# A norm whose second tile's products go ahead of the first tile's turning, and a mixer whose heads come out earlier and whose first result is turned by its roots

## The chip, the core and the metric

The kernel runs on one core of a Trainium2 chip. The core has five engines with a queue each. TensorE (PE in the profile) multiplies and turns, VectorE (DVE) and ScalarE (ACT) work on rows, GpSimd (POOL) helps out, and SyncE (SP) issues transfers. The engines meet only at semaphores. The metric is the device time of one execution in microseconds, smaller is better, and the median of three runs stands for a kernel.

## The reference, cut to what matters

Two transformer blocks follow each other on 256 tokens of width 1024. The change touches two places. The first lies between the first block's output product and its retrieval layer:

```python
x = x + mod[:, 2] * (concat(ret_lat, diff_lat) @ w_out)
h2 = modulate(x, norm2_g, mod[:, 3], mod[:, 4])   # rms_norm(x, g) * (1 + scale) + shift
q = (h2 @ w_query)                                # then scores, top 16, experts
```

The second is the mixer of the second block, with its two results ya and yb:

```python
v = layernorm(gelu(v));  mixed = einsum("hts,bcshd->bcthd", tril(w_s), v) + b_s
ya = rmsnorm(gelu(u) * mixed, gm_out_norm)        # first result
# second result: a state-space scan, 16 heads, in 4 groups of 4
y  = (scores * exp(segment sums)) @ (xs * dt) + xs * d_skip
yb = rmsnorm(y * silu(z)) * ssm_norm
h = h + concat(ya, yb) @ w_out
```

## The kernel before

Tokens lie in two tiles of 128 (i = 0 and 1), each a row of 1024 columns in `x[:, i, :]`. All weights stream from memory in halves of 128x1024 numbers, called units here. Of each unit ScalarE makes the rounded high part (`w_hi`) and VectorE the rest (`w_lo`, sometimes GpSimd does), and TensorE takes three products for every pair (`mm3`: high by high, high by low, low by high). The two parts live in a ring of four slots. `ahead(u)` on ScalarE and VectorE makes the parts of the units up to three beyond unit u, so a call with a later unit can only go when TensorE has used an older one. Each engine's program is written out by hand, and its order is the order in which it runs: an instruction that waits holds up everything behind it on its engine.

**The norm ahead of the queries.** `last_four` takes the last four units of the output product, for tile 0 and then for tile 1. Of tile 0's sum VectorE makes the new x (`add(0)`, four operations of 512 columns), ScalarE the mean square (`halves_squared`, `squares`), and VectorE the reciprocal root and with it a diagonal matrix (`inverse`). `turn_normed(i)` on TensorE multiplies the tile by that diagonal, which turns it and norms it in one, in eight 128x128 products. `normed_scaled` takes the result out of the banks with gain and shift, even blocks on VectorE and odd ones on ScalarE; `normed_highs` and `normed_lows` make the high and low part in `HX`. The query products (`feat_half`) need both tiles.

**The mixer.** While TensorE takes the 24 units of the gMLP products (`U_IN2`) and the 16 of the output product (`U_OUT2`), the rest of the mixer is fitted in beside them by the table `SIDE`. Row n of it names the steps that every engine does behind unit n: `beside` of TensorE, ScalarE and VectorE look up their own part of each name. Names that matter: `dec n` is four VectorE operations that make the exponents of head group n, `exp n` their exponential on ScalarE, `mt n` the masked matrix (VectorE), `heads` the products of four heads (TensorE). `y 0` takes the first eight heads out of banks 4 and 5 (VectorE). `gm i` are the eight products of the gating for tile i (TensorE), which use the same banks and so wait for `y 0`; `gmu i` multiplies them with u (VectorE). `usq`, `uvar`, `uroot` and `uscale` make the reciprocal roots of the first result and scale it by them, and `ubt n` turns block n of it on TensorE for the output product; `ubh` and `ubl` split the block into parts. The line that turns is

```python
ins = e.transpose(PB[b][:, i * 128:(i + 1) * 128], src(i), ident)
```

`fsc[:, 2, :]` is a piece of memory for two 128x128 diagonals; the norms use it as `dgn`.

Of the kernel before, what the change touches and what calls it, by code (L numbers as in the profile page):

```python
# [308 lines left out]
def group_done(g):  # L309
# [7 lines left out]
TB_DIFF, TB_RET, TB_U, TB_Y = 16, 20, 24, 32  # L317
# [20 lines left out]
    [("vc", 0)],  # L338
    [("vc", 1)],
    [("heads", 4), ("xd", 0)],  # L340
    [("xd", 1), ("dec", 2)],
    [("exp", 2), ("y", 0)],
    [("gm", 0), ("gmu", 0)],
    [("mt", 2)],
    [("gm", 1), ("gmu", 1)],
    [("usq", 0), ("dec", 3), ("uvar", 0), ("uroot", 0)],
# [16 lines left out]
N_PEER, N_F1, N_MIX, N_F2, N_PLE, N_END = range(6)  # L363
# [21 lines left out]
def program(nc, wall, keys_d, cols_d, rows_d, bigrows_d, crow_d, wmod_d, dist_d, x_d, ctx_d, pT_d, gws_d, out_d, n_chunks):  # L385
    assert n_chunks * 2 == U_END
    with ExitStack() as es:
# [22 lines left out]
        fsc = sb("fsc", 3, 256)  # L410
# [374 lines left out]
        def bank_of(n):  # L785
# [3 lines left out]
            for first, banks in ((TB_Y, (4, 5, 6, 7)), (TB_RET, (4, 5, 7, 6)), (TB_DIFF, (0, 1, 2, 3))):  # L789
                if n >= first:  # L790
                    return banks[(n - first) % len(banks)], n - len(banks) if n - first >= len(banks) else None

        def block_bank(n):
            if n < TB_DIFF:
                return PB[4 + n % 4 // 2][:, n % 2 * 256:n % 2 * 256 + 256]
            return PB[bank_of(n)[0]][:, 0:256]
# [66 lines left out]
        def tensor_program(e):  # L863
# [7 lines left out]
                mm(o, l[0], r[1], False, False)  # L871
                return mm(o, l[1], r[0], False, stop)

            def block(n, src, nt=2):

                b, old = bank_of(n)
                if old is not None:
                    t.wait_ge(s_fl, old + 1)
                for i in range(nt):
                    ins = e.transpose(PB[b][:, i * 128:(i + 1) * 128], src(i), ident)  # L880
                t.did(ins, s_tr)

            def mod_block(n):
# [164 lines left out]
            def last_four(us, banks, lhs, j, after=None):  # L1048

                for n in range(4):  # L1050
                    ins = tok_half(us[n], 0, banks, lambda i: lhs(n, i), False, n == 3)
                    if after is not None:
                        after(n)
                t.did(ins, s_t0)
                for n in range(4):
                    if n == 3 and j == N_PEER:
                        turn_normed(0)
                    if n == 2 and j in (N_F1, N_MIX, N_F2, N_PLE):
                        t.wait_ge(s_res, result(j, 0, 1))
                        turn_rows(0, range(4))  # L1060
                    t.did(tok_half(us[n], 1, banks, lambda i: lhs(n, i), False, n == 3), s_used)

            def turn_normed(i):

# [224 lines left out]
            def beside(name, n):  # L1289
# [35 lines left out]
                elif name == "gm":  # L1325
                    t.wait_ge(s_v2, 2)
                    t.wait_ge(s_set, 4)
                    t.wait_ge(s_y, 2)
                    for hb in range(2):
                        if n:  # L1330
                            t.wait_ge(s_um, hb + 1)
                        for k in range(4 * hb, 4 * hb + 4):
                            ins = mm(PB[4 + hb][:, (k % 4) * 128:(k % 4 + 1) * 128], gw[:, k, :],
                                     m_v[:, n, k * 128:(k + 1) * 128], True, True)
                        t.did(ins, s_gm)
                elif name == "ubt":
                    t.wait_ge(s_un, 2)
                    t.wait_ge(s_xs, 4)
                    t.wait_ge(s_uvz, 10)
                    block(TB_U + n, lambda i: m_u[:, i, n * 128:(n + 1) * 128])  # L1340
                elif name == "ybt":
                    t.wait_ge(s_yn, 4)
                    t.wait_ge(s_fl, TB_Y)
                    block(TB_Y + n, lambda i: m_y[:, i, n * 128:(n + 1) * 128])
# [48 lines left out]
        def scalar_program(e):  # L1393
# [45 lines left out]
                if meanwhile is not None:  # L1439
                    meanwhile(1)  # L1440

            def halves_squared(j, i, scr_):
                for hf in range(2):
                    a.wait_ge(s_res, result(j, i, hf))
                    act(scr_, x[:, i, hf * 512:(hf + 1) * 512], ACT.Square, scale=1.0 / 32,
                        acc=rs[:, 2 * i + hf:2 * i + hf + 1])
                    if hf == 0:
                        a.wait_ge(s_set, 1)
                        act(part[:, i:i + 1], rs[:, 2 * i:2 * i + 1], ACT.Identity, bias=epsc)

            def squares(j, i, scr_):

                halves_squared(j, i, scr_)
                act(root_[:, i:i + 1], rs[:, 2 * i + 1:2 * i + 2], ACT.Sqrt, bias=part[:, i:i + 1], sig=s_std)

            def normed_scaled(i):
# [12 lines left out]
            def normed(last, scr_):  # L1469

                squares(N_PEER, 0, scr_)
                ahead(last - 2)
                normed_scaled(0)
                normed_highs(0)
                squares(N_PEER, 1, scr_)
                ahead(last - 1)
                normed_scaled(1)
                normed_highs(1)
                ahead(last)
# [356 lines left out]
        def vector_program(e):  # L1836
# [110 lines left out]
            def normed(last, add):  # L1947
# [1 line left out]
                v.wait_ge(s_t0, N_PEER + 1)  # L1949
                add(0)  # L1950
                inverse(N_PEER, 0)
                ahead(last - 2)
                normed_scaled(0)
                v.wait_ge(s_used, used(last))
                add(1)
                normed_lows(0)
                inverse(N_PEER, 1)
                normed_scaled(1)
                normed_lows(1)
                ahead(last)  # L1960
# [472 lines left out]
            def beside(name, n):  # L2433
# [67 lines left out]
                elif name == "uscale":  # L2501
                    v.wait_ge(s_us, 1)
                    rcp(lnst[:, 4:6], lnst[:, 4:6])
                    for i in range(2):
                        ts(m_u[:, i, :], m_u[:, i, :], lnst[:, 4 + i:5 + i], sig=s_un)
                elif name in ("ubl", "ybl"):
                    low((TB_U if name == "ubl" else TB_Y) + n)
                elif name == "yz":
# [237 lines left out]
```

## Time and profile before

| | |
|---|---|
| median of three runs | 1744.52 us (1743.62 to 1744.93) |
| profiled execution | 1747.22 us, its span 1745.5 us |
| TensorE busy | 1649.3 us, 94% of the span |
| VectorE busy | 1251.7 us, 72% |
| ScalarE busy | 909.6 us, 52% |
| the norm ahead of the queries | 262 to 282 us from the span's start |
| the mixer's middle | 1424 to 1457 us |

The profile is of one execution. "Idle before" in a row is the time in which the engine did nothing ahead of the instruction, and behind the arrow stands the work whose end released it. The granted clock of TensorE (PEclk) is a share of full speed: 1.00 is 2.4 GHz and 0.50 is 1.2 GHz.

### The profile page before, as it was taken

What the parts mean: (1) busy time and instruction counts of PE and PEld (TensorE: products, weight loads), DVE (VectorE), ACT (ScalarE), POOL (GpSimd) and SP (SyncE); (2) the same over time, 40 slices, a digit from 0 to 9 for tenths busy, and PEclk for the clock granted to TensorE, in tenths of its full rate; (3) what the DMA queues carried; (4) which work ended last, traced back from release to release, by engine and by line L of the source; (5) the groups of instructions that cost most, each with busy time, mean ns of one, the idle gap of its engine ahead of it and who ended that gap; (6) DMA issues with size and microseconds to landing.
All of it is one profiled execution on the core that took longest, in us unless ns stands there. A gap on an engine that the chain in (4) does not pass through costs nothing.

```text
span 1745.5 us, 28968 instructions
## 1 busy us (share of the span) xinstructions
PE 1649.3 (94%) x11496; PEld 1480.5 (85%) x11496; DVE 1251.7 (72%) x2028; ACT 909.6 (52%) x1192; POOL 84.2 (5%) x50
## 2 busy tenths in 40 slices
PE   6898887999999999999999999999998979999997
PEld 6776667999999888788999999899998768899996
DVE  5886665899988899987666665655557887655556
ACT  4354555555555554554444444544446757544446
POOL 0100002622000000000000000000000000000000
PEclk9898898999999999999999999999999999999999
DMA  6744233346555555556556455454544533554551
GB/s 258 276 169 157 97 112 139 149 161 212 184 185 192 181 191 207 209 209 246 207 215 217 187 218 186 149 204 179 194 173 154 209 129 121 190 202 173 193 188 75
DMA packets 53418, 318.52 MB, mean 182 GB/s; under 512 B 5953, under 2 KB 6113, under 8 KB 19362
## 3 DMA queue, kind: packets, MB, share of 16 engines
q1 hardware_dynamic: 52098, 310.60, 48.8%
q0 software_dynamic: 1184, 6.05, 0.9%
q8 instruction: 91, 1.49, 0.3%
q14 instruction: 45, 0.37, 0.1%
HBM read 307.17 MB, written 9.47 MB: 181 GB/s over the span
## 4 chain that ended last, share of the span: by engine, by line
PE 73%; DVE 17%; ACT 6%; issue 1%; DMA 1%; SPq 0%; DVEq 0%; ACTq 0%
PE pb L867 73%; DVE w_lo L1843 4%; DVE ar L1843 4%; ACT ar L1403 3%; ACT w_hi L1403 2%; DVE ar L1855 1%; DVE ar L2207 1%; DMA raw<-in_wall 1%; DVE ar L2005 1%; DVE ar L2204 1%; ACT L1403 1%; DVE raw L2005 1%; DVE ar L2002 1%; DVE ar L2211 1%; DVE sm L2070 0%
## 5 line engine op out<-in xcount | busy, mean ns | idle before, releaser
L1843 DVE TENSOR_TENSOR w_lo<-raw,w_hi 128x1024 fp32r<-128x1024 f32 x467 | 572.3, 1226 | 254.0 <-ACT w_hi L1403 228.7
L867 PE MATMUL pb<-HX,w_hi 128*128 128x256 f32 x3904 | 717.0, 285 | 13.0 <-DVE w_lo L1843 6.0
L1403 ACT ACTIVATE w_hi<-raw 128x1024 fp32r<-128x1024 f32 x498 | 529.2, 1063 | 308.2 <-PE pb L867 285.3
L867 PEld LDWEIGHTS pb<-HX,w_hi 128*128 128x128 f32 x3904 | 614.9, 193 | 20.1 <-DVE w_lo L1843 5.2
L867 PE MATMUL pb<-HX,w_lo 128*128 128x256 f32 x1952 | 554.2, 284 | 0.0
L867 PE MATMUL pb<-w_hi,HC 128*128 128x512 f32 (+1 forms) x1648 | 526.5, 391 | 4.2 <-DVE HC L1855 3.3
L867 PEld LDWEIGHTS pb<-HX,w_lo 128*128 128x128 f32 x1952 | 376.4, 193 | 0.0
L867 PEld LDWEIGHTS pb<-w_hi,HC 128*128 128x128 f32 x1648 | 309.5, 188 | 68.4 <-DVE HC L1855 2.7
L867 PE MATMUL pb<-w_lo,HC 128*128 128x512 f32 (+1 forms) x824 | 320.4, 389 | 0.0
L1843 DVE TENSOR_TENSOR ar<-ar 128x512 bf16<-128x512 bf16 (+8 forms) x470 | 247.8, 564 | 53.1 <-ACT ar L1403 33.5
L1403 ACT ACTIVATE ar<-pb 128x512 f32<-128x512 f32 (+3 forms) x200 | 112.6, 563 | 256.9 <-PE pb L867 155.0
L867 PE MATMUL pb<-w_hi,HX 128*128 128x512 f32 x512 | 177.6, 414 | 11.5 <-DVE HX L1843 3.3
L867 PEld LDWEIGHTS pb<-w_lo,HC 128*128 128x128 f32 x824 | 155.5, 189 | 29.0
L867 PE MATMUL pb<-ar 128*128 128x64 bf16 (+3 forms) x1960 | 128.4, 224 | 22.5 <-ACT ar L1403 8.3
L867 PEld LDWEIGHTS pb<-ar 128*128 128x128 bf16 (+2 forms) x1960 | 107.0, 121 | 45.4 <-issue 26.1
L867 PEld LDWEIGHTS pb<-w_hi,HX 128*128 128x128 f32 x512 | 101.6, 198 | 38.0 <-issue 7.2
L867 PE MATMUL pb<-w_lo,HX 128*128 128x512 f32 x256 | 103.8, 405 | 0.0
L1403 ACT ACTIVATE HC<-ar 128x512 fp32r<-128x512 f32 x87 | 55.1, 634 | 93.2 <-PE pb L867 51.9
L1843 DVE TENSOR_TENSOR HC<-ar,HC 128x512 fp32r<-128x512 f32 x87 | 60.3, 693 | 44.9 <-ACT HC L1403 41.3
L2594 POOL TENSOR_TENSOR w_lo<-raw,w_hi 128x1024 fp32r<-128x1024 f32 x31 | 76.1, 2454 | 156.6 <-ACT w_hi L1403 116.4
L1403 ACT ACTIVATE ar<-ar 128x512 f32<-128x512 f32 (+6 forms) x85 | 50.4, 593 | 49.1 <-DVE ar L1850 17.1
L867 PEld LDWEIGHTS pb<-w_lo,HX 128*128 128x128 f32 x256 | 50.8, 198 | 9.5
(145 smaller groups left out, 700.6 us busy)
## 6 DMA issues: line engine op xcount, KB each, us to landing
raw<-in_wall SPq DMA_DIRECT2D x257, 1024.0 KB, 4.8
ar<-in_wmod SPq DMA_DIRECT2D x24, 512.0 KB, 3.7
act_keep<-ar SPq DMA_DIRECT2D x28, 256.0 KB, 5.6
ar<-act_keep SPq DMA_DIRECT2D x28, 256.0 KB, 5.0
x<-in_wmod SPq DMA_DIRECT2D x8, 512.0 KB, 5.3
ar<-in_bigrows POOLq DMA_DIRECT2D x2, 1024.0 KB, 5.0
ar<-acs_keep POOLq DMA_DIRECT2D x2, 1024.0 KB, 7.3
ar<-in_crow SPq DMA_DIRECT2D x2, 512.0 KB, 6.5
```

The source lines that it names most:

```text
L867: return e.matmul(o, l, r, start=start, stop=stop, skip_group_check=True)
L1403: a.did(e.activation(out, in_, func, scale=scale, **kw), sig)
L1843: v.did(e.tensor_tensor(out, a_, b_, op), sig)
L1855: v.did(e.scalar_tensor_tensor(out, a_, s_, b_, op0, op1), sig)
L2002: v.did(e.scalar_tensor_tensor(junk, w, 1.0, crow_ctx, MUL, MUL, accum_out=modT[:, n, 1:2]))
L2005: v.did(e.scalar_tensor_tensor(w, w, 1.0, c_, MUL, MUL, accum_out=modT[:, n, 0:1]), s_modv)
L2204: v.did(e.max(vals[:, c_], src))
L2207: v.did(e.max_index(idx[:, c_], vals[:, c_], src))
L2211: v.did(e.match_replace(src, vals[:, c_], src, NEG))
L2594: p.did(e.tensor_tensor(w_lo[:, made % NH, :], raw_half(w), w_hi[:, made % NH, :].bitcast(F32), SUB), s_lop)
```

## The change

Three things are changed.

1. The norm. TensorE does `turn_normed(0)` behind all products of tile 1 and no longer ahead of the last unit's. VectorE adds tile 1 (`add(1)`) ahead of scaling tile 0's turned rows, makes the second diagonal ahead of tile 0's low part, and the low part of a weight (`ahead(last - 2)`) behind both. ScalarE squares the first half of tile 1 ahead of scaling tile 0, and the second half behind it.
2. The table `SIDE`. `y 0` stands one row earlier and ahead of `dec 2`; `exp 2` stands one row later.
3. The first result is no longer multiplied by its reciprocal roots on VectorE. Two 128x128 diagonals (`dgu`) are made of them, and `ubt` multiplies each block by the diagonal in place of turning it with the identity. That is 16 products in place of 16 transposes.

```diff
-    [("xd", 1), ("dec", 2)],
-    [("exp", 2), ("y", 0)],
-    [("gm", 0), ("gmu", 0)],
+    [("xd", 1), ("y", 0)],
+    [("dec", 2)],
+    [("gm", 0), ("exp", 2), ("gmu", 0)],
...
+        dgu = fsc[:, 2, :].rearrange("p (i t) -> p i t", i=2)
...
+                    place = PB[b][:, i * 128:(i + 1) * 128]
+                    if diag is None:
+                        ins = e.transpose(place, src(i), ident)
+                    else:
+                        ins = mm(place, src(i), diag[:, i, :], True, True)
...
                 for n in range(4):
-                    if n == 3 and j == N_PEER:
-                        turn_normed(0)
...
                     t.did(tok_half(us[n], 1, banks, lambda i: lhs(n, i), False, n == 3), s_used)
+                if j == N_PEER:
+                    turn_normed(0)
...
-                    block(TB_U + n, lambda i: m_u[:, i, n * 128:(n + 1) * 128])
+                    block(TB_U + n, lambda i: m_u[:, i, n * 128:(n + 1) * 128], diag=dgu)
...
                 squares(N_PEER, 0, scr_)
                 ahead(last - 2)
+                halves_squared(N_PEER, 1, scr_, (0,))
                 normed_scaled(0)
+                squares(N_PEER, 1, scr_, (1,))
                 normed_highs(0)
-                squares(N_PEER, 1, scr_)
...
                 inverse(N_PEER, 0)
-                ahead(last - 2)
-                normed_scaled(0)
                 v.wait_ge(s_used, used(last))
                 add(1)
+                normed_scaled(0)
+                inverse(N_PEER, 1)
                 normed_lows(0)
-                inverse(N_PEER, 1)
+                ahead(last - 2)
                 normed_scaled(1)
...
-                        ts(m_u[:, i, :], m_u[:, i, :], lnst[:, 4 + i:5 + i], sig=s_un)
+                        ts(dgu[:, i, :], ident, lnst[:, 4 + i:5 + i], sig=s_un)
```

VectorE at the norm, before. Banks pb0 and pb1 hold tile 0 and pb2 and pb3 tile 1; the reciprocal and the row with `cols` behind it are `inverse`.

```order
L1867 RECIPROCAL sm<-sm 128x1
L1848 TENSOR_SCALAR fsc<-cols,sm 128x128
L1843 TENSOR_TENSOR w_lo<-raw,w_hi 128x1024
L1850 TENSOR_SCALAR ar<-pb0,sm,modT 128x128 x4
L1843 TENSOR_TENSOR ar<-pb2,ar 128x512
L1843 TENSOR_TENSOR x<-x,ar 128x512
L1843 TENSOR_TENSOR ar<-pb3,ar 128x512
L1843 TENSOR_TENSOR x<-x,ar 128x512
L1843 TENSOR_TENSOR HX<-ar,HX 128x4x128 x2
L1867 RECIPROCAL sm<-sm 128x1
L1848 TENSOR_SCALAR fsc<-cols,sm 128x128
L1850 TENSOR_SCALAR ar<-pb2,sm,modT 128x128 x4
```

The same place in the changed kernel:

```order
L1875 RECIPROCAL sm<-sm 128x1
L1856 TENSOR_SCALAR fsc<-cols,sm 128x128
L1851 TENSOR_TENSOR ar<-pb2,ar 128x512
L1851 TENSOR_TENSOR x<-x,ar 128x512
L1851 TENSOR_TENSOR ar<-pb3,ar 128x512
L1851 TENSOR_TENSOR x<-x,ar 128x512
L1858 TENSOR_SCALAR ar<-pb0,sm,modT 128x128 x4
L1875 RECIPROCAL sm<-sm 128x1
L1856 TENSOR_SCALAR fsc<-cols,sm 128x128
L1851 TENSOR_TENSOR HX<-ar,HX 128x4x128 x2
L1851 TENSOR_TENSOR w_lo<-raw,w_hi 128x1024
L1858 TENSOR_SCALAR ar<-pb2,sm,modT 128x128 x4
```

Tile 1's additions now stand right behind the first diagonal, and between the second diagonal and the scaling of tile 1 (`ar<-pb2`) now stand tile 0's low part and a weight's low part.

VectorE in the mixer, before, from the second `xd` on. The three rows behind it and the 128x1024 one are `dec 2`, the rows with pb4 and pb5 and no `cols` are `y 0`, and those with `cols` are `gmu 0`.

```order
L1843 TENSOR_TENSOR ar<-ar,rows 128x1024
L1843 TENSOR_TENSOR ar<-ar 128x4
L1843 TENSOR_TENSOR ar<-ar 128x4x2x128
L1843 TENSOR_TENSOR ar<-ar 128x512
L1848 TENSOR_SCALAR ar<-ar 128x1024
L1843 TENSOR_TENSOR w_lo<-raw,w_hi 128x1024
L1843 TENSOR_TENSOR ar<-pb4,ar 128x512
L1843 TENSOR_TENSOR ar<-pb5,ar 128x512
L1843 TENSOR_TENSOR w_lo<-raw,w_hi 128x1024
L1855 SCALAR_TENSOR_TENSOR ar<-pb4,cols,ar 128x128 x4
```

And in the changed kernel:

```order
L1851 TENSOR_TENSOR ar<-ar,rows 128x1024
L1851 TENSOR_TENSOR ar<-pb4,ar 128x512
L1851 TENSOR_TENSOR ar<-pb5,ar 128x512
L1851 TENSOR_TENSOR w_lo<-raw,w_hi 128x1024
L1851 TENSOR_TENSOR ar<-ar 128x4
L1851 TENSOR_TENSOR ar<-ar 128x4x2x128
L1851 TENSOR_TENSOR ar<-ar 128x512
L1856 TENSOR_SCALAR ar<-ar 128x1024
L1851 TENSOR_TENSOR w_lo<-raw,w_hi 128x1024
L1863 SCALAR_TENSOR_TENSOR ar<-pb4,cols,ar 128x128 x4
```

The two rows that empty banks 4 and 5 now stand ahead of `dec 2` and of one low part; the low parts and `gmu 0` keep their places.

ScalarE in the mixer, before, from the outputs of the u products on. The 128x1536 row is `exp 2`.

```order
L1403 ACTIVATE ar<-pb,sm 128x512 x2
L1403 ACT_TABLE_LOAD
L1403 ACTIVATE ar<-ar 128x1536
L1403 ACTIVATE w_hi<-raw 128x1024 x4
L1403 ACT_TABLE_LOAD
```

And in the changed kernel:

```order
L1410 ACTIVATE ar<-pb,sm 128x512 x2
L1410 ACTIVATE w_hi<-raw 128x1024
L1410 ACT_TABLE_LOAD
L1410 ACTIVATE ar<-ar 128x1536
L1410 ACTIVATE w_hi<-raw 128x1024 x3
L1410 ACT_TABLE_LOAD
```

One high part of a weight now stands ahead of the exponential, the number of instructions is the same.

## Rows read from the trace of the kernel before

**Rows 1.** The page: the chain of work that ended last, shares by engine.

```profile
PE 73%; DVE 17%; ACT 6%; issue 1%; DMA 1%; SPq 0%; DVEq 0%; ACTq 0%
```

**Rows 2.** Timeline, TensorE, norm: start, duration (us), what, idle before.

```profile
266.60 2.02 PE L867 MATMUL pb<-fsc,x 128*128 128x128 f32 x16 [0.58 <-DVE fsc L1848]
268.38 0.48 PE L867 MATMUL pb<-w_hi,HC 128*128 128x512 f32 x1
...
275.14 3.75 PE L867 MATMUL pb<-fsc,x 128*128 128x128 f32 x16 [5.13 <-DVE fsc L1848]
282.03 0.77 PE L867 MATMUL pb<-HX,w_hi 128*128 128x256 f32 x2 [3.14 <-DVE HX L1843]
```

**Rows 3.** Timeline, VectorE, norm.

```profile
268.47 1.75 DVE L1850 TENSOR_SCALAR ar<-pb,sm,modT 128x128 f32<-128x128 f32 x4
270.33 0.69 DVE L1843 TENSOR_TENSOR ar<-pb,ar 128x512 f32<-128x512 f32 x1
...
273.12 1.29 DVE L1843 TENSOR_TENSOR HX<-ar,HX 128x512 fp32r<-128x512 f32 x2
...
274.70 0.29 DVE L1848 TENSOR_SCALAR fsc<-cols,sm 128x128 f32<-128x128 f32 x1
```

**Rows 4.** Timeline, ScalarE, norm: the second half's square and root of tile 1.

```profile
273.23 0.63 ACT L1403 ACTIVATE ar<-x 128x512 f32<-128x512 f32 x1 [0.40 <-DVE x L1843]
...
273.99 0.30 ACT L1403 ACTIVATE sm<-sm 128x1 f32<-128x1 f32 x1
```

**Rows 5.** Timeline, TensorE, mixer.

```profile
1432.90 3.75 PE L867 MATMUL pb<-ar 128*128 128x128 f32 x16 [6.64 <-DVE ar L1843]
...
1442.69 1.95 PE L867 MATMUL pb<-ar 128*128 128x128 f32 x16
1444.39 0.48 PE L867 MATMUL pb<-w_hi,HX 128*128 128x512 f32 x1
...
1449.97 2.79 PE L867 MATMUL pb<-ar 128*128 128x64 f32 x24
...
1457.11 1.09 PE L880 MATMUL pb<-cols,ar 128*128 128x128 f32 x8 [1.54 <-DVE ar L1848]
```

**Rows 6.** Timeline, VectorE, mixer.

```profile
1427.02 2.15 DVE L1843 TENSOR_TENSOR ar<-ar 128x4 f32<-128x4 f32 x3
1429.21 0.69 DVE L1848 TENSOR_SCALAR ar<-ar 128x1024 f32<-128x1024 f32 x1
1430.00 1.23 DVE L1843 TENSOR_TENSOR w_lo<-raw,w_hi 128x1024 fp32r<-128x1024 f32 x1
1431.33 1.42 DVE L1843 TENSOR_TENSOR ar<-pb,ar 128x512 f32<-128x512 f32 x2
...
1439.25 1.76 DVE L1843 TENSOR_TENSOR ar<-ar 128x1536 f32<-128x1536 f32 x1
...
1443.78 2.36 DVE L1855 SCALAR_TENSOR_TENSOR ar<-pb,cols,ar 128x128 f32<-128x128 f32 x8 [1.29 <-PE pb L867]
...
1455.52 1.54 DVE L1848 TENSOR_SCALAR ar<-ar 128x1024 f32<-128x1024 f32 x2
```

**Rows 7.** Timeline, ScalarE, mixer: the first result's root, the next high part.

```profile
1452.65 0.20 ACT L1403 ACTIVATE ar<-ar 128x2 f32<-128x2 f32 x1
1452.89 1.06 ACT L1403 ACTIVATE w_hi<-raw 128x1024 fp32r<-128x1024 f32 x1
```

**Rows 8.** Stretches: busy (instructions) of PE, PEld, DVE, ACT, POOL; PEclk; DMA; GB/s.

```profile
233.60:236.00 2.40, 0.00 (x0) 0.00 (x1) 2.33 (x6) 2.11 (x4) 1.04 (x2) 1.00 0.01 2
236.70:240.00 3.30, 3.30 (x10) 2.53 (x9) 1.10 (x3) 2.84 (x4) 0.00 (x0) 0.50 0.42 159
274.30:287.80 13.50, 9.52 (x43) 9.29 (x44) 7.52 (x13) 6.17 (x10) 0.00 (x0) 0.50 0.21 58
288.00:300.00 12.00, 12.00 (x103) 12.00 (x102) 1.89 (x12) 5.79 (x8) 7.95 (x4) 1.00 0.74 280
```

**Rows 9.** A stretch behind the first turning in the mixer, same columns.

```profile
1457.10:1485.00 27.90, 27.22 (x142) 23.09 (x143) 21.03 (x29) 20.53 (x31) 0.00 (x0) 1.00 0.39 144
```

More of the change, by code:

```diff
@@ L872, in mm3, with block @@
                 return mm(o, l[1], r[0], False, stop)
-            def block(n, src, nt=2):
+            def block(n, src, nt=2, diag=None):
                 b, old = bank_of(n)
@@ L879, in block @@
                 for i in range(nt):
-                    ins = e.transpose(PB[b][:, i * 128:(i + 1) * 128], src(i), ident)
+                    place = PB[b][:, i * 128:(i + 1) * 128]
[3 more added lines that the diff above has]
+                        ins = mm(place, src(i), diag[:, i, :], True, True)
                 t.did(ins, s_tr)
@@ L1440, in softplus_parts, with halves_squared @@
                     meanwhile(1)
-            def halves_squared(j, i, scr_):
-                for hf in range(2):
+            def halves_squared(j, i, scr_, halves=(0, 1)):
+                for hf in halves:
                     a.wait_ge(s_res, result(j, i, hf))
@@ L1449, in halves_squared, with squares @@
                         act(part[:, i:i + 1], rs[:, 2 * i:2 * i + 1], ACT.Identity, bias=epsc)
-            def squares(j, i, scr_):
-                halves_squared(j, i, scr_)
+            def squares(j, i, scr_, halves=(0, 1)):
+                halves_squared(j, i, scr_, halves)
                 act(root_[:, i:i + 1], rs[:, 2 * i + 1:2 * i + 2], ACT.Sqrt, bias=part[:, i:i + 1], sig=s_std)
```

## The prediction

> **What bounds the kernel now.** I read the page first. Its chain of work puts 73% of the span on TensorE, 17% on VectorE and 6% on ScalarE [rows 1], so TensorE is the bound, and time is to be had only where it stands still or runs at its lower clock. So I went to its timeline at the two places of the change. At the norm it stands still for 5.13 us ahead of turning tile 1 and for 3.14 us ahead of the first query products [rows 2]. In the mixer it stands still for 6.64 us ahead of the first gating products and for 1.54 us ahead of the first turning of the first result; the former wait is for VectorE's `y 0`, the latter for the scaling by the roots [rows 5]. Then I read the granted clock. It is 0.50, which is 1.2 GHz, from 274.3 to 287.8 us, and the engine had stood still from 270.0 us before it fell [rows 2, 8]. The same 16 records of the gating products take 3.75 us behind the long wait and 1.95 us later [rows 5], so there the clock had fallen too. Behind both places TensorE works without a pause: 12.00 of 12 us, and 27.22 of 27.9 us [rows 8, 9]. What comes earlier there should therefore come earlier at the end, one for one.
>
> **The norm.** The reader can follow the moved chain with the durations of the rows.
>
> The last six products of tile 1 no longer stand behind the turning. The product before them ended at 266.0 us (266.60 less 0.58), and the six took 1.6 us (from 268.38 to the 270.0 at which the wait of 5.13 us began). Part of that is the ramp of a first product, so they should end at about 267.4 us. VectorE's `add(1)` can start there in place of 270.33; it takes 2.8 us (270.33 to 273.1) and ends at 270.3 [rows 2, 3].
>
> ScalarE squares the first half at about 268.9, then scales tile 0's odd blocks (1.5 us, taken like VectorE's 1.75 us for the even ones less a little), which holds it to 271.6. Then comes the second half's square and root, 1.06 us by the old timeline (273.23 to 274.29): 272.7. VectorE has scaled its blocks by 272.1 (270.3 plus 1.75). Reciprocal and diagonal end at 273.2, and TensorE turns tile 1 from 273.4 us in place of 275.14 [rows 2 to 4]. That is 1.7 us.
>
> Two moved pieces are now late instead. Tile 0's low part (1.29 us) ran ahead of the second diagonal; now it and a weight's low part (1.23 us) run behind it, to 276.0, beside the turning of tile 1. VectorE's scaling of tile 1 starts then and ends at 277.8. Before, TensorE's restart came 3.1 us behind the end of the turning (275.14 plus 3.75, then 3.14 idle). If the turning takes 3.75 us again, it ends at 277.2 and the restart falls at 280.3; if it takes 2.02 us as tile 0's did [rows 2], VectorE's 277.8 decides, and with a high part and a low part of about 0.65 us each the restart falls at 279.4. So this is worth 1.7 to 2.6 us; I take **2.0**, nearer to the lower, because TensorE still stands still for some 4 us ahead of tile 1's turning.
>
> The clock stayed low for 5.8 us of work behind the restart (282.03 to 287.8), and for at least 3.3 us in another place [rows 2, 8]. At 0.50 work takes at most twice as long. If the low stretch behind the restart lasts 4.6 us, midway, 1.2 us less are spent at half speed, which is worth 0.5 us. The bounds are 0 and 2.9 us (all of the 5.8 gone). I take **0.5**.
>
> **The mixer.** Here the path between the two waits of TensorE lies on VectorE, and I add it up from 1427.0 us, where `dec 2` started [rows 6]. The new order is `y 0` (1.42), a low part (1.23), `dec 2` (2.15 and 0.69), a low part, `gmu 0` (2.36, as `gmu 1`), a low part, `mt 2` (1.76), a low part, `gmu 1` (2.36), a low part, `dec 3` (2.84). That is 1.42 + 5 x 1.23 + 2 x 2.84 + 2 x 2.36 + 1.76 = 19.7 us of work, and with 0.1 us for most hand-overs (1429.90 to 1430.00) 20.7: VectorE is through `dec 3` at 1447.8. Behind it stand a small operation (0.2), the root on ScalarE (0.20), the next high part (1.06) [rows 7], its low part (1.23), the reciprocal (0.2) and now two diagonals of 0.29 us each [rows 3] in place of two full rows, 1.54 us in all [rows 6]. These are 3.5 us, 3.8 with hand-overs. TensorE can turn the first result at **1451.7** in place of 1457.11, 5.4 us earlier.
>
> Is TensorE there by then? The gating products start behind `y 0` at 1428.6. They take 1.70 us to the next start (1442.69 to 1444.39), twice; a unit takes 2.79 us (half of 1444.39 to 1449.97), and there are five; four heads take some 2.6 us and wait for `gmu 1`, which ends at 1443.5 [rows 5, 6]. That gives 1449.0, so VectorE decides and TensorE idles for 2.7 us. All of the slow stretch behind the old wait of 6.64 us is already in the 5.4 us: it is ahead of the turning, and the new path runs past it on VectorE.
>
> On ScalarE `exp 2` now waits for `dec 2` until 1432.7, and the high part of the unit three on follows it at 1435.4. TensorE needs that unit at about 1440.5. That cover is 5 us; `mt 2` needs `exp 2` only at 1437.9. I cost the move at nothing.
>
> The turning itself becomes dearer. 16 records of 128x128 take 1.95 us and the 8 of the transposes 1.09 us, and eight products of a diagonal with a tile are 16 records (at the norm, 2.02 us) [rows 2, 5]. So the first four blocks cost **0.9 us** more, all on the path, since TensorE is the bound behind them [rows 9], and the other four blocks cost **0.9 us** more later.
>
> FP8 and Floating Point Precision, section TensorE Precision Notes, of the Trainium skill says that true FP32 takes four passes through the array, and TensorE: Matmul & The Clock Gate, section Terms, that the transpose mode makes FP32 four times as fast. By that rule a product would cost four times a transpose, about 4.4 us for a group of eight and not 1.95, and the whole turning would cost 6.5 us more and not 1.7. The norm's rows are of just such products, and they show twice [rows 2]; I go by the rows.
>
> The new idle time of 2.7 us ahead of the turning can cost clock. Elsewhere TensorE did nothing for 2.4 us at 1.00, and the next 3.3 us ran at 0.50 [rows 8]. That costs at most half of 3.3 us, 1.7, or nothing where the clock holds. I take **0.8**, the middle.
>
> **The sum.** Norm 2.0 + 0.5; mixer 5.4 - 0.9 - 0.9 - 0.8 = 2.8; together 5.3 us. The profiled execution took 1747.22 us (span 1745.5), 2.7 above the median of 1744.52. It becomes 1741.9, and the median **1739.2**.
>
> **The rivals.** What this measurement can tell from no change is about 0.2%, 3.5 us, so 1741.0 is the border of faster.
>
> *The forecast* as above, its own range 1736.0 to 1741.0. Its gain is at the best 2.6 + 2.9 at the norm and 5.4 - 1.8 in the mixer, 9.1 us, and 1735.4. Chance 0.68.
>
> *The mixer's wait moves.* If one step that I took as free holds TensorE or VectorE for 3 us (the heads behind `mt 2`, or the high parts behind the late `exp 2`), the first turning falls at 1454.7 and the total gain is 2.3 to 3.8 us: 1740.7 to 1742.2. For it speaks that VectorE's new path has no idle time left in it for 20 us; against it the 5 us of cover above. Chance 0.12, half of it faster.
>
> *The norm gives nothing.* Restart and clock as before, if the low parts that now stand ahead of tile 1's scaling take back what the diagonal won. That needs 1.7 us more there than I found, and the total gain is 2.8 us: 1741.7. Chance 0.08, a quarter of it faster since the mixer may do better than its middle.
>
> *The diagonal products cost four times a transpose.* Then 6.5 in place of 1.8 us, gain 0.6: 1743.9. That it would be so for the mixer's tile while the norm's is twice has nothing in the rows for it; chance 0.04.
>
> *Nothing moves on the path*, because TensorE waits later for something that is not moved, such as a transfer: 1744.5. The full stretches behind both places [rows 8, 9] speak against it. Chance 0.04.
>
> *Slower, through the clock.* At the norm the clock stayed at 0.50 for 13.5 us over two idle stretches [rows 8]. In the mixer there would be two short ones now (2.3 us ahead of the gating, 2.7 us ahead of the turning). If each left the clock low for 13.5 us, TensorE would lose up to 6.7 us twice. Against the 6.1 us of gain without my clock terms (2.0 + 5.4 - 1.8, and 0.5) the time would be 1744.5 - 6.1 + 13.4 = 1751.8. It decides from about 12 us at half speed on, against none that the mixer's rows show behind a wait as short as 1.54 us [rows 9]. Chance 0.04.
>
> **Chances and range.** Faster: 0.68 + 0.06 + 0.02 = 0.76. Same: 0.06 + 0.06 + 0.04 + 0.04 = 0.20. Slower 0.04. The range goes from the forecast's best (1736.0) over the moved wait and the empty norm to 1742.3, and leaves about 0.15 outside.
>
> **What the changed profile would show.** `add(1)` on VectorE starts within 0.2 us of the end of TensorE's last product for tile 1; the second turning starts about 4 us behind the end of the first; the restart of the query products comes about 13.5 to 14.3 us behind the end of tile 1's third unit (16.0 before). In the mixer the wait ahead of the gating is about 2.3 us and its 16 records take about 2 us; the wait ahead of the first turning is about 2.7 us and its diagonals are two rows of 0.29 us; its records are 16 and take about 2 us. I would be wrong if the wait at the first turning were much longer, if new waits stood between 1457 and 1490 us on TensorE (the second result's turning has its own chain there), or if the granted clock stayed low beyond 4 us behind either.

## The result, and the profile after

| | before | after |
|---|---|---|
| median, timed side by side | 1744.53 us (1742.88 to 1745.89, 10 runs) | 1740.18 us (1736.71 to 1741.24, 10 runs) |
| profiled execution, its span | 1747.22, 1745.5 us | 1740.01, 1738.2 us |

The ratio is 0.9973, with a 95% interval of 0.9964 to 0.9981: 4.35 us less by the medians, where 5.3 us less had been forecast. The interval lies wholly below one, so the changed kernel is faster, by less than half a per cent.

The page of the changed kernel, shares of the chain of work by engine, hardly differs from [rows 1]:

```profile
PE 73%; DVE 18%; ACT 6%; issue 1%; DMA 1%; SPq 0%; DVEq 0%; ACTq 0%
```

So the two places have to be read by themselves. The timeline of TensorE in the changed kernel, first the norm and then the mixer (start, duration, what, idle before), answers to [rows 2, 5]:

```profile
265.54 1.95 PE L870 MATMUL pb<-fsc,x 128*128 128x128 f32 x16
271.64 3.25 PE L870 MATMUL pb<-fsc,x 128*128 128x128 f32 x16 [4.16 <-DVE fsc L1856]
278.04 0.48 PE L870 MATMUL pb<-HX,w_hi 128*128 128x256 f32 x2 [3.14 <-DVE HX L1851]
...
1423.39 2.02 PE L870 MATMUL pb<-ar 128*128 128x128 f32 x16 [2.44 <-DVE ar L1851]
...
1438.44 2.86 PE L870 MATMUL pb<-ar 128*128 128x64 f32 x24 [0.27 <-DVE ar L1863]
...
1446.38 3.67 PE L870 MATMUL pb<-fsc,ar 128*128 128x128 f32 x16 [2.27 <-DVE fsc L1856]
...
1455.38 2.79 PE L870 MATMUL pb<-ar 128*128 128x64 f32 x24
```

The wait ahead of tile 1's turning fell from 5.13 to 4.16 us and the one ahead of the gating from 6.64 to 2.44. The one ahead of the first result's turning grew from 1.54 to 2.27. Its 16 records took 3.67 us, close to the 3.75 that the gating's took before: the low clock is not gone, it has changed place.

VectorE at the norm: first the reciprocal root of tile 0 in the kernel before, then the changed kernel, which answers to [rows 3]:

```profile
265.97 0.16 DVE L1867 RECIPROCAL sm<-sm 128x1 f32<-128x1 f32 x1 [1.12 <-ACT sm L1403]
```

```profile
264.28 0.16 DVE L1875 RECIPROCAL sm<-sm 128x1 f32<-128x1 f32 x1 [1.12 <-ACT sm L1410]
...
265.74 0.69 DVE L1851 TENSOR_TENSOR ar<-pb,ar 128x512 f32<-128x512 f32 x1 [0.98 <-PE pb L870]
...
271.21 0.29 DVE L1856 TENSOR_SCALAR fsc<-cols,sm 128x128 f32<-128x128 f32 x1
...
273.19 1.23 DVE L1851 TENSOR_TENSOR w_lo<-raw,w_hi 128x1024 fp32r<-128x1024 f32 x1
274.53 1.75 DVE L1858 TENSOR_SCALAR ar<-pb,sm,modT 128x128 f32<-128x128 f32 x4
```

From the reciprocal root to the second diagonal it is 6.93 us, against 8.73 before (265.97 to 274.70). The weight's low part at 273.19 now stands right ahead of tile 1's scaling, and the scaling ends at 276.28. TensorE had ended its turning at 274.9 (278.04 less 3.14), and ScalarE had waited for that:

```profile
274.94 1.51 ACT L1410 ACTIVATE ar<-pb,modT,sm 128x128 f32<-128x128 f32 x4 [1.42 <-PE pb L870]
276.53 1.29 ACT L1410 ACTIVATE HX<-ar 128x512 fp32r<-128x512 f32 x2
```

ScalarE's half of the scaling ends at 276.45, 0.2 us behind VectorE's, and the high parts follow it. So in this execution the turning at 1.2 GHz sets the restart by way of ScalarE, and VectorE is close behind it; with a turning at full clock it is VectorE, as fill_both shows below.

VectorE in the changed kernel, mixer, answers to [rows 6]:

```profile
1421.83 1.42 DVE L1851 TENSOR_TENSOR ar<-pb,ar 128x512 f32<-128x512 f32 x2
...
1439.66 2.15 DVE L1851 TENSOR_TENSOR ar<-ar 128x4 f32<-128x4 f32 x3
...
1444.18 1.23 DVE L1851 TENSOR_TENSOR w_lo<-raw,w_hi 128x1024 fp32r<-128x1024 f32 x1 [1.36 <-ACT w_hi L1410]
1445.51 0.17 DVE L1875 RECIPROCAL ar<-ar 128x2 f32<-128x2 f32 x1
1445.71 0.61 DVE L1856 TENSOR_SCALAR fsc<-cols,ar 128x128 f32<-128x128 f32 x2
```

VectorE runs from `y 0` to the diagonals with one pause of over 1 us, the 1.36 us for the high part of a weight. The two diagonals take 0.61 us; the two full rows took 1.54.

Stretches of the changed kernel (busy time and instructions of PE, PEld, DVE, ACT, POOL; granted clock; DMA share; GB/s), which answer to [rows 8, 9]:

```profile
265.50:272.10 6.60, 2.44 (x21) 2.24 (x20) 5.22 (x11) 4.54 (x12) 0.00 (x0) 1.00 0.00 0
272.30:275.50 3.20, 2.60 (x13) 2.30 (x11) 2.91 (x6) 1.68 (x4) 0.00 (x0) 0.50 0.00 0
275.70:278.90 3.20, 0.86 (x7) 0.90 (x8) 2.14 (x5) 2.96 (x6) 0.00 (x0) 1.00 0.00 0
279.10:282.40 3.30, 3.30 (x18) 3.30 (x17) 3.06 (x4) 1.05 (x1) 0.00 (x0) 0.50 0.41 104
1423.40:1446.30 22.90, 20.44 (x116) 17.32 (x116) 20.02 (x35) 14.24 (x16) 0.00 (x0) 1.00 0.31 116
1446.40:1449.70 3.30, 3.30 (x15) 3.30 (x16) 1.39 (x2) 3.00 (x4) 0.00 (x0) 0.50 0.79 318
```

TensorE works at 1.2 GHz from 272.3 to 275.5 us and from 279.1 to 282.4, each time behind an idle time, and again for 3.3 us behind the wait of 2.27 us at the turning. The gating, behind a wait of 2.44 us, was granted 2.4 GHz. The diagonals' products are thus dear for two reasons at once: there are twice as many records, and in this execution they ran at half the clock.

### The profile page after: what moved, and what is told of

It is laid out like the page before. It is cut to its first block, busy times and chain, and to the rows that moved or that the text cites. A ratio compares the mean times of both kernels' runs of the same rounds, so it can differ in the third digit from the quotient of the medians.

```text
span 1738.2 us, 29000 instructions
## 1 busy us (share of the span) xinstructions
PE 1647.9 (95%) x11512; PEld 1479.5 (85%) x11512; DVE 1250.9 (72%) x2028; ACT 907.9 (52%) x1192; POOL 83.8 (5%) x50
## 4 chain that ended last, share of the span: by engine, by line
PE 73%; DVE 18%; ACT 6%; issue 1%; DMA 1%; SPq 0%; DVEq 0%; ACTq 0%
PE pb L870 73%; DVE w_lo L1851 4%; DVE ar L1851 4%; ACT ar L1410 3%; DVE ar L1863 2%; ACT w_hi L1410 2%; DVE ar L2215 1%; DMA raw<-in_wall 1%; DVE ar L2013 1%; DVE ar L2212 1%; DVE raw L2013 1%; ACT L1410 1%; DVE ar L2010 1%; DVE ar L2219 1%; DVE sm L2078 0%
```

## The experiments

To compare traces I cut each at six starts: the turning of tile 0, the restart of the query products, the first `xd` on VectorE, the gating, the first turning, and the last four heads behind it. The first `xd` in the kernel before and in the changed one:

```profile
1423.18 1.22 DVE L1843 TENSOR_TENSOR ar<-ar,rows 128x1024 f32<-128x1024 f32 x1
```

```profile
1417.92 1.22 DVE L1851 TENSOR_TENSOR ar<-ar,rows 128x1024 f32<-128x1024 f32 x1
```

The table gives the microseconds between the starts, with the last piece reaching to the end of the span. A reader who takes them from the rows will find 0.01 us of rounding, and up to 0.05 in the last piece, since the span is printed to 0.1 us. "Median" is the time of the run, with the ratio to the kernel before on the same chip and its 95% interval. The kernel before had medians of 1744.65 us beside the first group of runs (norm_only, order_only, diag_only, norm_order), 1744.00 beside the second (after_again, fill_both and the two dec3_late) and 1745.66 beside the third (the other four, on another chip), so compare the ratios rather than the medians.

| kernel | to restart | to `xd` | to gating | to turning | to heads | to end | median, ratio (interval) |
|---|---|---|---|---|---|---|---|
| before | 15.43 | 1141.15 | 9.72 | 24.22 | 6.40 | 281.98 | |
| after | 12.50 | 1139.88 | 5.48 | 22.98 | 9.00 | 282.87 | 1740.18, 0.9973 (0.9964 to 0.9981) |
| after_again | 12.27 | 1140.69 | 5.48 | 22.96 | 8.99 | 282.91 | 1739.86, 0.9972 (0.9961 to 0.9983) |
| after_third | 12.28 | 1139.88 | 5.48 | 22.97 | 7.37 | 282.95 | 1739.18, 0.9958 (0.9944 to 0.9972) |
| norm_only | 12.26 | 1140.70 | 9.73 | 24.10 | 6.41 | 281.98 | 1741.28, 0.9981 (0.9972 to 0.9990) |
| order_only | 15.43 | 1139.04 | 5.48 | 23.90 | 7.94 | 281.93 | 1741.25, 0.9981 (0.9972 to 0.9990) |
| diag_only | 15.43 | 1141.08 | 9.72 | 23.35 | 7.38 | 282.93 | 1746.23, 1.0006 (0.9997 to 1.0015) |
| norm_order | 12.27 | 1140.54 | 5.48 | 23.90 | 9.23 | 283.49 | 1738.89, 0.9965 (0.9951 to 0.9978) |
| norm_order_again | 12.55 | 1139.16 | 5.48 | 23.91 | 6.41 | 283.56 | 1738.71, 0.9967 (0.9955 to 0.9978) |
| fill_both | 12.26 | 1139.95 | 5.48 | 23.82 | 7.28 | 282.84 | 1739.15, 0.9965 (0.9952 to 0.9979) |
| dec3_late | 12.26 | 1139.86 | 5.48 | 23.29 | 8.71 | 285.03 | 1741.89, 0.9984 (0.9975 to 0.9993) |
| dec3_late_fill | 12.27 | 1139.06 | 5.48 | 23.08 | 8.72 | 284.65 | 1740.55, 0.9977 (0.9966 to 0.9988) |
| norm_order_fill | 12.39 | 1139.72 | 5.48 | 23.91 | 6.40 | 281.98 | 1737.25, 0.9954 (0.9940 to 0.9968) |
| pool_fill | 12.53 | 1140.07 | 5.48 | 23.91 | 6.39 | 282.04 | 1737.30, 0.9953 (0.9938 to 0.9967) |

What lies ahead of tile 0's turning is left out of it: it starts between 263.7 and 266.6 us, and not by the change alone. In the kernels with part 1 it also stands behind six more products, so the first piece is to be compared with care.

**norm_only**: part 1 of the change alone.

```diff
+                if j == N_PEER:
+                    turn_normed(0)
```

> Only the norm's part of the change. My theory (each place adds its own gain): add(1) starts behind the last product, the restart of the query products comes 2.3 us earlier against the turning of tile 0 than before, and with a shorter low stretch of the clock the median is 2 to 3 us below before, 1741.5 to 1742.5. Rival (the norm gives nothing, all of the gain is the mixer's): within 0.7 us of before.

Measured: 3.4 us less, a little more than expected. Only the first piece of the table is plainly another one, 3.17 us shorter, and the mixer's waits are as before. Part of the 3.17 is only that the turning itself starts later: from the reciprocal root to the restart it takes 13.52 us (265.05 to 278.57) against 16.06, 2.54 less.

**order_only**: part 2 alone, the table `SIDE`.

```diff
+    [("xd", 1), ("y", 0)],
+    [("dec", 2)],
+    [("gm", 0), ("exp", 2), ("gmu", 0)],
```

> Only the table: y 0 ahead of dec 2, exp 2 a row later. Theory: the wait ahead of the gating products shrinks from 6.6 to 2.4 us and the first turning, still by transposes of a scaled result, starts 4.5 us earlier than before against dec 2's neighbour xd 1 (5.4 with the diagonals, less the 0.93 us of the longer scaling); the median is 2.5 to 4.5 us below before, 1740.0 to 1742.0. Rival (the reordering only moves the wait to the turning, and the roots' diagonals are what frees it): less than 1.5 us below before.

Measured: 3.4 us less. From `xd` to the turning it takes 29.38 us and not 33.94, 4.56 less, as expected, of which the piece behind the turning gives back 1.54 through the clock. Here the clock fell at both places: the 16 records of the gating took 3.56 us and the 8 transposes 1.97.

**diag_only**: part 3 alone, the products with diagonals.

```diff
+                        ins = mm(place, src(i), diag[:, i, :], True, True)
...
+                        ts(dgu[:, i, :], ident, lnst[:, 4 + i:5 + i], sig=s_un)
```

> Only the diagonals in place of scaling and transposes. Theory: VectorE is through 0.93 us earlier, the first four blocks cost TensorE 0.9 us more and the other four another 0.9, so the median is 0.5 to 1.5 us above before, 1745.0 to 1746.0, less than the measurement can tell. Rival (the diagonals give their 0.93 us and the products hide): about 1 us below before.

Measured: 1.0006, an interval on both sides of one. TensorE of this kernel at the first turning, the four heads behind it, and the second turning:

```profile
1455.87 2.05 PE L869 MATMUL pb<-fsc,ar 128*128 128x128 f32 x16 [0.59 <-DVE fsc L1854]
...
1463.25 2.79 PE L869 MATMUL pb<-ar 128*128 128x64 f32 x24
...
1469.49 1.05 PE L869 MATMUL pb<-fsc,ar 128*128 128x128 f32 x8
```

At full clock the 16 records take 2.05 us, where the 8 transposes took 1.09 [rows 5]. The turning comes 0.87 us sooner, the first four blocks cost 0.97 more and the others 0.95 more: from `xd` to the end 323.38 us against 322.32. By the trace part 3, taken alone, costs 1 us; the times can't tell it from nothing.

**norm_order**: parts 1 and 2 without part 3.

```diff
-                        ts(dgu[:, i, :], ident, lnst[:, 4 + i:5 + i], sig=s_un)
+                        ts(m_u[:, i, :], m_u[:, i, :], lnst[:, 4 + i:5 + i], sig=s_un)
```

> The change without its diagonals (first result scaled on VectorE, turned by transposes). Theory: 0.8 us less than the full change needs, so 5 to 6 us below before, 1738.5 to 1739.5, and its profile shows the first turning 0.9 us later against xd 1 and each later unit again 0.8 us earlier than with the diagonals. Rival (the diagonals earn their keep): at or above the full change, 4 us or less below before.

**norm_order_again** is the same kernel, a second time.

> Norm and table without the diagonals, beside the full change. Theory (the products cost TensorE 0.9 and 0.9 us and give 0.93; but a wait of 3.2 us ahead of the transposes, in place of 2.3, lets the clock fall for longer): within 1 us of the full change, on either side. Rival (the diagonals plainly pay or plainly cost): more than 1.5 us apart.

Measured: ratios of 0.9965 and 0.9967, some 6 us less. TensorE at the first turning of the first of the two:

```profile
1446.56 1.97 PE L880 MATMUL pb<-cols,ar 128*128 128x128 f32 x8 [3.17 <-DVE ar L1849]
```

The wait is 0.9 us longer than in the changed kernel (3.17 against 2.27), since full rows are scaled, but the transposes take 1.97 us even at the low clock, less than the products' 3.67. The turning comes 0.9 us later, as expected. What was expected behind it did not come: the last piece is 283.49 and 283.56 us, longer and not shorter than the changed kernel's 282.87. In both traces the clock fell once more, behind the last four heads, which it does in none of the three traces of the changed kernel; in norm_order:

```profile
1459.40:1462.70 3.30, 3.30 (x9) 2.56 (x9) 1.23 (x1) 0.21 (x1) 0.00 (x0) 0.50 0.32 45
```

(In norm_order_again it was from 1456.1 to 1459.4 us.) So from `xd` to the end these two traces take 322.10 and 319.36 us, the three of the changed kernel 320.33, 320.34 and 318.77. Beside part 2, the traces do not show that part 3 loses.

**after_again** and **after_third** are the changed kernel, beside the others.

> The changed kernel once more, beside the others of this job. Both theories: 3.5 to 5 us below before, 1739.5 to 1741.2.

> The changed kernel a third time, beside the next three. 3.5 to 5 us below before.

Measured: ratios 0.9972 and 0.9958; the latter is 7.3 us less, more than the 5 expected at most. TensorE of after_third at the gating and at the turning, and the stretch behind the gating:

```profile
1424.12 3.48 PE L870 MATMUL pb<-ar 128*128 128x128 f32 x16 [2.43 <-DVE ar L1851]
...
1447.09 2.05 PE L870 MATMUL pb<-fsc,ar 128*128 128x128 f32 x16 [1.28 <-DVE fsc L1856]
```

```profile
1427.20:1458.00 30.80, 28.90 (x169) 25.00 (x168) 25.45 (x42) 23.46 (x27) 0.00 (x0) 1.00 0.39 137
```

Here the clock fell at the gating (16 records in 3.48 us) and not at the turning. TensorE lost 1.46 us there, and its wait ahead of the turning was that much shorter, 1.28 us: the turning came 22.97 us behind the gating, as before, because VectorE decides. The fall at the gating costs nothing; the same fall at the turning costs 1.6 us (7.37 against 9.00 in the table). Which of the two it is changes between executions of one and the same kernel, though order_only had both.

**fill_both**: the changed kernel, in which TensorE multiplies the identity by itself into a bank that is not in use while it would stand still. Nothing of the computation is changed.

```diff
+            for _ in range(18):
+                mm(PB[4][:, 0:128], ident, ident, True, True)
             turn_normed(1)
+            for _ in range(13):
+                mm(PB[4][:, 0:128], ident, ident, True, True)
...
+                    if n == 0:
+                        for _ in range(10):
+                            mm(PB[6][:, 0:128], ident, ident, True, True)
```

> The changed kernel with idle products of the identity with itself on TensorE: 18 ahead of turning tile 1, 13 behind it, 10 ahead of the first turning in the mixer; nothing reads them. Theory (what is left of the three waits costs mostly by the lower clock that follows them): the granted clock stays at 1.00 through both places, turning tile 1 takes 2 us and not 3.25, the first turning in the mixer 2 us and not 3.7, the restart of the queries runs at full speed; 3 to 4.5 us below the changed kernel, 1736 to 1737.5. Rival (the clock is lowered by something else, or the waits themselves are all of the cost): the same as the changed kernel within 1 us.

Measured: 1739.15, and the expected gain is missed. TensorE of this kernel at the norm and at the mixer's turning, and two stretches:

```profile
267.65 4.18 PE L870 MATMUL pb<-cols 128*128 128x128 f32 x36
271.97 2.02 PE L870 MATMUL pb<-fsc,x 128*128 128x128 f32 x16
...
278.13 0.47 PE L870 MATMUL pb<-HX,w_hi 128*128 128x256 f32 x2 [1.24 <-DVE HX L1858]
...
1445.16 2.40 PE L870 MATMUL pb<-cols 128*128 128x128 f32 x20
1447.39 1.95 PE L870 MATMUL pb<-fsc,ar 128*128 128x128 f32 x16
```

```profile
265.90:300.00 34.10, 32.73 (x278) 32.41 (x277) 21.25 (x66) 20.42 (x34) 12.91 (x6) 1.00 0.44 155
433.50:436.80 3.30, 3.30 (x18) 3.30 (x17) 2.99 (x5) 1.01 (x1) 0.00 (x0) 0.50 0.23 25
```

The products did hold the clock, at 1.00 through the whole norm. The second turning took 2.02 us and not 3.25, and yet the restart came 12.26 us behind the first turning, as in norm_only and 0.24 us sooner than in the changed kernel, for VectorE had the low part and the scaling to do first: ScalarE's high parts waited 1.10 us for it. And in the three kernels that fill the norm the clock fell once at about 431 to 433 us, in none of the others, behind a wait of 1.9 us that the changed kernel has there as well. The 3.3 us at 1.2 GHz that the restart lost stand there again. The piece up to `xd` is 1139.95 us, 1140.07 and 1139.06 in the three kernels that fill the norm and 1139.04 to 1141.15 in the others, so a gain of the filled norm isn't shown. In the mixer the ten products stood in the way themselves: TensorE came to them late, since the clock had fallen at the gating (its 16 records took 3.53 us), and they ran until the turning at 1447.39 while VectorE had its diagonals by 1446.48. The turning came 23.82 us behind the gating and not 22.98, which gives back 0.8 us.

**dec3_late**: norm_order with `dec 3` and `exp 3` one row later, to let VectorE reach the scaling sooner.

```diff
-    [("usq", 0), ("dec", 3), ("uvar", 0), ("uroot", 0)],
-    [("heads", 8), ("uscale", 0), ("exp", 3)],
-    [("mt", 3), ("ubt", 0), ("ubt", 1), ("ubt", 2), ("ubt", 3)],
+    [("usq", 0), ("uvar", 0), ("uroot", 0)],
+    [("heads", 8), ("uscale", 0), ("dec", 3)],
+    [("ubt", 0), ("ubt", 1), ("ubt", 2), ("ubt", 3), ("exp", 3)],
```

(`mt 3` goes to the row of `ubh 0`.)

> norm and table as changed, no diagonals, and dec 3 on VectorE moved from ahead of the first result's roots to behind its scaling; exp 3 and mt 3 follow it. Theory (VectorE's string between the gating products and the first turning sets the turning's start): the wait ahead of the first turning shrinks from 3.2 us to 1.5 us or less, the clock holds there, and the median is 2 to 3.5 us below the kernel with norm and table alone (1738.9), 1735.5 to 1737. Rival (the ScalarE chain of squares and root decides): less than 1 us below it.

**dec3_late_fill** is the same with the products of fill_both at the norm, 18 and 13, and none in the mixer.

> The one before with the idle products at the norm (18 and 13). Theory: both gains add, another 2 to 3 us, 1733 to 1735. Rival: no more than the one before.

Measured: 1741.89 and 1740.55. Both miss what was expected and have a higher ratio than norm_order, though their intervals overlap its own, that of dec3_late only just. TensorE of dec3_late at the turning and at the last four heads, and the stretch behind:

```profile
1445.56 1.09 PE L880 MATMUL pb<-cols,ar 128*128 128x128 f32 x8 [1.52 <-DVE ar L1849]
...
1454.27 3.65 PE L867 MATMUL pb<-ar 128*128 128x64 f32 x24 [2.17 <-DVE ar L1844]
```

```profile
1456.30:1463.00 6.70, 5.87 (x18) 4.85 (x18) 3.46 (x5) 1.97 (x3) 0.00 (x0) 0.50 0.33 100
```

The turning came 0.6 us sooner, but `mt 3` was late and the heads now wait 2.17 us for it, and the clock is low for 6.7 us soon behind it. The two waits compete for the same VectorE.

**norm_order_fill**: norm_order with 12 products of the identity ahead of the first turning.

```diff
+                    if n == 0:
+                        for _ in range(12):
+                            mm(PB[6][:, 0:128], ident, ident, True, True)
```

> The same with 12 idle products of the identity in the 3.2 us ahead of the first turning in the mixer. Theory: the clock holds there; from xd to the first four heads behind the turning 35.8 us and not 37.5 to 38.6, and the stretch from there to the end 282.0 and not 282.9; 2 to 2.6 us below the full change in its own profile, 1737.3 to 1738 in the median. Rival: the clock falls somewhere else for as long, and the median is the full change's.

Measured: 1737.25, 0.9954. TensorE of this kernel at the turning, and the whole mixer as one stretch:

```profile
1442.36 2.84 PE L867 MATMUL pb<-cols 128*128 128x128 f32 x24
1445.69 1.09 PE L880 MATMUL pb<-cols,ar 128*128 128x128 f32 x8 [0.48 <-DVE ar L1852]
```

```profile
1421.80:1458.40 36.60, 35.18 (x209) 30.58 (x210) 30.57 (x46) 23.74 (x27) 0.00 (x0) 1.00 0.37 132
```

The clock stays at 1.00, the turning takes 1.09 us, and the pieces are those that were expected (35.79 us from `xd` to the heads, 281.98 from there to the end), and from `xd` to the end it takes 317.77 us, against 320.33, 320.34 and 318.77 in the three traces of the changed kernel. With pool_fill this is the fastest kernel that I found. Its interval overlaps those of the changed kernel and of norm_order, so that by the time alone it isn't shown to be faster; by the traces its mixer is, by 1.0 to 2.6 us.

**pool_fill**: norm_order_fill with the norm filled too, and with the low part of the first query weight on GpSimd.

```diff
-LO_POOL |= {HALF_OF["win", p, h] for p in (0,) for h in range(4)}
+LO_POOL |= {HALF_OF["win", p, h] for p in (0,) for h in range(4)} | {U_QUERY}
```

> The same, with the idle products at the norm too (18 and 12), and the first query unit's low part made on GpSimd, which stands idle there, and no longer on VectorE between tile 0's low part and tile 1's scaling. Theory (with the clock held, VectorE's string decides the restart): from turning tile 0 to the restart 11.0 to 11.3 us in place of 12.3, and the low clock behind the restart gone; 1 to 2.5 us below the kernel before it, 1735.5 to 1736.8. Rival (the ScalarE string decides the restart, or a fall of the clock later takes it back, as at 433 us in the kernel with idle products): no more than 0.5 us below it.

Measured: 1737.30, as without it, and 12.53 us to the restart where 11.0 to 11.3 were expected. GpSimd and VectorE of this kernel:

```profile
263.67 2.35 POOL L2602 TENSOR_TENSOR w_lo<-raw,w_hi 128x1024 fp32r<-128x1024 f32 x1 [30.78 <-ACT w_hi L1410]
```

```profile
263.89 0.69 DVE L1851 TENSOR_TENSOR ar<-pb,ar 128x512 f32<-128x512 f32 x1 [0.97 <-PE pb L867]
264.62 1.95 DVE L1851 TENSOR_TENSOR x<-x,ar 128x512 f32<-128x512 f32 x1
...
267.33 0.69 DVE L1851 TENSOR_TENSOR x<-x,ar 128x512 f32<-128x512 f32 x1
```

The 1.23 us did leave VectorE, and from the second diagonal on it paid: 5.59 us to the restart (270.63 to 276.22), where fill_both took 6.59 (271.54 to 278.13). But VectorE's addition beside GpSimd's row took 1.95 us and the same one behind it 0.69, and the second diagonal was 1.27 us late for it. The one took back the other.

## Why the prediction was right, point by point

The direction, the places and most sizes hold. One term, the clock at the turning, was set at a middle that never occurs, and the term for the clock behind the restart isn't shown to come from the change.

- *Norm, predicted 2.0 us.* From the reciprocal root to the restart it took 16.06 us before and 13.76 after: 2.30, within 1.7 to 2.6. `add(1)` started at 265.74, 0.2 us behind TensorE's last product, and the second turning 4.16 us behind the end of the first. The prediction gave both ends: TensorE's turning decides where it is slow, VectorE's scaling where it is fast. Here it took 3.25 us, and the two chains ended 0.2 us apart; in fill_both, with a turning of 2.02 us, VectorE decided and the restart came no more than 0.24 us sooner.
- *Clock behind the restart, predicted 0.5.* In this pair the low stretch behind the restart went from 5.8 us [rows 8] to 3.3 us. But in after_again it was 5.2 us, and in order_only, which has the old norm, 3.3:

```profile
276.20:281.40 5.20, 5.20 (x24) 5.20 (x25) 4.46 (x5) 1.99 (x2) 0.00 (x0) 0.50 0.42 126
```

```profile
280.40:283.70 3.30, 3.30 (x17) 3.30 (x17) 3.06 (x4) 1.06 (x2) 0.00 (x0) 0.50 0.33 62
```

  So the shorter stretch isn't shown to be the change's. The whole piece up to `xd` is 1.27 us shorter in this pair, but it varies between 1139.0 and 1141.2 us over kernels that have the same code in it. It goes with the time at 1.2 GHz in it: 6.8 us in order_only and norm_order_again (1139.04, 1139.16), 12.0 to 12.7 us in norm_only and before (1140.70, 1141.15). That is 0.30 to 0.36 us lost for each microsecond at the low clock, below the one half that I had as the most. Some of these low stretches lie far behind the norm and come and go between executions of the same kernel; this one is in after and not in after_third:

```profile
1118.80:1122.00 3.20, 2.75 (x13) 2.75 (x14) 2.72 (x7) 2.33 (x7) 0.00 (x0) 0.50 0.30 128
```

```profile
1100.00:1140.00 40.00, 37.38 (x241) 33.21 (x240) 29.04 (x39) 25.30 (x38) 0.00 (x0) 1.00 0.44 155
```

  How much of the 1.27 us the change gives, the runs don't settle.
- *Mixer, the turning 5.4 us earlier.* From `xd` to the turning 33.94 us became 28.46: 5.48. order_only gives 4.56 of it and diag_only 0.87; they add. The wait ahead of the turning is for VectorE, 2.27 us where 2.7 stood.
- *Products of diagonals, 0.9 and 0.9.* 0.97 and 0.95 in diag_only. By an estimate from the factor of four that the Trainium skill gives for the transpose mode (TensorE: Matmul & The Clock Gate, section Terms) they would have cost 3.3 us more for each half; the traces of this case show 1.9 times a transpose (2.05 against 1.09 us), and the measurement decides.
- *Clock behind the new idle time, predicted 0.8 with bounds 0 and 1.7.* **This is the term that was mis-sized.** It is 1.6 where the clock falls at the turning (after, after_again) and 0 where it falls at the gating (after_third). It is no middle but one of the two, and with 0 the sum would have been 6.1. In norm_order it is 2.8, with the clock low for 5.9 us.
- *The sum.* The profiled executions differ by 7.2 us, of which 1.7 lie ahead of the norm and are nothing of the change. The other 5.6 are 2.30 + 1.27 + 5.48 - 2.60 - 0.9. The medians differ by 4.35, and the ratios of the three runs of this kernel (0.9973, 0.9972, 0.9958) give 4.7 to 7.3 us on 1744.5. The forecast of 5.3 lies within. That the traced sum is so near the forecast is in part luck: the piece behind the restart gave 0.8 us more than its term, which isn't shown to be the change's, and the clock at the turning took 0.8 us more than its own, which the next executions may or may not repeat.

Of the rivals, the mixer's wait did not move: the four heads waited 0.27 us, and the high parts beside the late `exp 2` held nobody. dec3_late shows what it is like where it does. Slower through the clock would have needed 12 us at half speed; there were 3.3.

What the prediction did not say, though its own terms gave it: part 3 taken alone saves 0.9 us of VectorE and costs twice 0.9 on TensorE, so it should lose. It is in the sum with its costs, and I never asked for the sum without it. The trace of diag_only shows that loss where the table is the old one. In the full change it isn't settled. norm_order and norm_order_again have a lower ratio than two of the three runs of the full change, not than the third, and from `xd` to the end the traces without the diagonals (322.10, 319.36) are no shorter than those with them (320.33, 320.34, 318.77), because of the further fall of the clock behind the heads. Where the clock falls neither at the turning nor behind it, part 3 again costs 1.0 us: 318.77 in after_third, 317.77 in norm_order_fill.

Open: why the clock fell at about 431 to 433 us in the kernels that fill the norm, what decides in one execution whether it falls at the gating or at the turning, and why without the diagonals it fell again behind the last four heads.

## What to carry to other kernels

Price every part of a change on its own, and also in the company of the others: an operation that frees the waiting engine and loads the one that bounds the kernel can lose, and in diag_only 0.9 us won on VectorE cost 1.9 on TensorE. A fall of the clock costs most where the engine that falls is the one that decides next: 1.6 us at the mixer's turning, nothing at the gating, 0.24 us at most for the second turning of the norm. Empty products in an idle time paid, by the traces, at the mixer's turning; at the norm no gain is shown, and where TensorE came to them late they held up the work behind them. Before work goes to a helper engine, look at what the busy engine runs at the same moment.

## What the runs showed of the hardware

- TensorE's clock fell to 1.2 GHz behind idle times of 2.27 us (after, at the turning) and 2.17 us (dec3_late), and behind 2.43 us in after_third, while behind 2.44 us at the same place in after it did not. Of the eleven traces with a wait of 2.40 to 2.45 us ahead of the gating it fell in five (after_third, order_only, norm_order_again, fill_both, dec3_late; the 16 records took 3.48 to 3.56 us) and held in six (2.02 us). Products of the identity by itself held it at 2.4 GHz: 34.1 us at 1.00 over the norm in fill_both. What decides between a fall and none at the same wait is open.
- A VectorE addition with both inputs in the on-chip memory took 1.95 us beside a GpSimd subtraction of 2.35 us, and 0.69 alone; it ended at 266.57, 0.55 us behind GpSimd's end at 266.02. The Trainium skill, SBUF — State Buffer, section "SBUF: two separate sides", says that such a pair takes turns at a shared port, the second standing still until the first is through; this trace agrees. The addition with one input in a bank, at 263.89, ran beside the same subtraction and took its usual 0.69 us.
